# Strassen's scheme for the feed-forward gate and up projections of a five-mixer network on one core

## The reference, cut to what matters

```python
D_MODEL, SEQ, DEPTH = 1024, 512, 2
D_FF = 2816                      # ceil(8 * 1024 / 3 / 256) * 256

def _swiglu(h, w_gate, w_up, w_down):
    g = h @ w_gate.astype(h.dtype)
    u = h @ w_up.astype(h.dtype)
    return (jax.nn.silu(g) * u) @ w_down.astype(h.dtype)

h = _rmsnorm(x, norm_ffn_g[layer])
x = x + _swiglu(h, ffn_w_gate[layer], ffn_w_up[layer], ffn_w_down[layer])
```

## Time and profile before

| What | Value |
|---|---|
| median of three runs | 1898.31 us |
| span of the profiled execution, first to last instruction | 1895.7 us |
| PE / PEld / DVE / ACT / POOL busy | 99% / 79% / 57% / 42% / 8% |
| the two feed-forward blocks, by the starts of their first and next units | 215.49 to 575.97 us and 818.74 to 1179.22 us |
| mean granted TensorE clock | 0.999 |
| HBM traffic | 91 GB/s over the span |

### The profile page before, as it was taken

The page is one execution under the profiler, slowest core; times in us unless marked ns, Lnnn a source line. Parts: engine busy times, 40 slices in busy tenths (PEclk is TensorE's granted clock), DMA queues, the critical chain, the costliest instruction groups (busy, mean ns, idle before and its releaser), DMA issues.

```text
span 1895.7 us, 25382 instructions
## 1 busy us (share of the span) xinstructions
PE 1883.0 (99%) x9078; PEld 1504.8 (79%) x9078; DVE 1079.8 (57%) x1730; ACT 793.5 (42%) x1271; POOL 154.5 (8%) x234
## 2 busy tenths in 40 slices
PE   9999999999999999999999999999999999999998
PEld 7887888888888777788888888876777887777777
DVE  7787644433456676744443446576666565656553
ACT  6476432222234444533312334255655244445442
POOL 3111000000000000000000000000002054432000
PEclk9999999999999999999999999999999999999999
DMA  7333333323332122232322232212313232332222
GB/s 252 115 93 122 100 100 100 115 73 100 100 100 75 59 66 66 80 100 90 110 100 83 95 109 89 69 45 62 94 57 91 85 95 80 85 84 84 82 89 73
DMA packets 53855, 173.78 MB, mean 92 GB/s; under 512 B 7392, under 2 KB 15712, under 8 KB 53776
## 3 DMA queue, kind: packets, MB, share of 16 engines
q1 hardware_dynamic: 47408, 162.62, 27.0%
q0 software_dynamic: 6368, 10.13, 2.3%
HBM read 168.51 MB, written 4.21 MB: 91 GB/s over the span
## 4 chain that ended last, share of the span: by engine, by line
PE 96%; DVE 1%; ACT 1%; DMA 1%; issue 1%; DVEq 0%; ACTq 0%; SPq 0%
PE ps L494 17%; PE ps L496 17%; PE ps L495 17%; PE sc L494 6%; PE sc L495 6%; PE sc L496 6%; PE tr L495 4%; PE tr L496 4%; PE tr L494 4%; PE ps L683 3%; PE tr L649 3%; PE sc L606 2%; PE ps L606 1%; PE sc L654 1%; PE ps L670 1%; DMA Wr<-in_w 1%
## 5 line engine op out<-in xcount | busy, mean ns | idle before, releaser
L1090 ACT ACTIVATE Wh<-Wr 128x1024 fp32r<-128x1024 f32 (+2 forms) x268 | 300.1, 1120 | 638.4 <-PE ps L496 284.2
L494 PE MATMUL ps<-Hl,Wh 128*128 128x512 f32 x1136 | 465.6, 410 | 0.0
L496 PE MATMUL ps<-Hh,Wh 128*128 128x512 f32 x1136 | 444.0, 391 | 0.0
L495 PE MATMUL ps<-Hh,Wl 128*128 128x512 f32 x1136 | 443.2, 390 | 0.0
L1550 DVE TENSOR_TENSOR Wl<-Wr,Wh 128x1024 fp32r<-128x1024 f32 (+2 forms) x268 | 352.2, 1314 | 139.5 <-ACT Wh L1090 138.2
L494 PEld LDWEIGHTS ps<-Hl,Wh 128*128 128x128 f32 x1136 | 213.4, 188 | 53.8 <-issue 11.1
L496 PEld LDWEIGHTS ps<-Hh,Wh 128*128 128x128 f32 x1136 | 213.3, 188 | 46.7
L495 PEld LDWEIGHTS ps<-Hh,Wl 128*128 128x128 f32 x1136 | 213.9, 188 | 39.4 <-issue 0.5
L494 PE MATMUL sc<-Hl,Wh 128*128 128x512 f32 x432 | 168.6, 390 | 0.0
L495 PE MATMUL sc<-Hh,Wl 128*128 128x512 f32 x432 | 168.1, 389 | 0.0
L496 PE MATMUL sc<-Hh,Wh 128*128 128x512 f32 x432 | 168.1, 389 | 0.0
(11 more groups left out here) (334 smaller groups left out, 2662.5 us busy)
## 6 DMA issues: line engine op xcount, KB each, us to landing
Wr<-in_w SPq DMA_DIRECT2D x228, 512.0 KB, 3.5
Wr<-in_w SPq DMA_DIRECT2D x32, 768.0 KB, 4.3
Wr<-in_w SPq DMA_DIRECT2D x16, 640.0 KB, 3.8
scr<-in_rpb POOLq DMA_DIRECT2D x128, 24.0 KB, 2.2
X<-in_x SPq DMA_DIRECT2D x8, 256.0 KB, 4.3
Wr<-in_wri SPq DMA_DIRECT2D x4, 512.0 KB, 3.5
out_t<-X SPq DMA_DIRECT2D x8, 256.0 KB, 2.4
scr<-d_rel POOLq DMA_DIRECT2D x8, 192.0 KB, 3.9
```

The lines of the kernel that those rows point to most:

```text
L494: pe.matmul(bank[:, 0:n], hi, rl[:, k, :], start=(k == 0), stop=False)
L495: pe.matmul(bank[:, 0:n], lo, rh[:, k, :], start=False, stop=False)
L496: return pe.matmul(bank[:, 0:n], hi, rh[:, k, :], start=False, stop=(k == kc - 1))
L1090: act.activation(place(Wh, slot, kc), place(Wr, slot, kc), ACT.Copy).then_inc(w_hi, 1)
```

## The change

A gate unit and an up unit of one hidden chunk are now one **pair**. With the weights as A11, A12 (gate, input chunks of even and of odd number), A21, A22 (up, the same) and the activations as B11, B12 (even chunks, left and right 256 tokens), B21, B22 (odd chunks), the four 128 x 256 results are made by seven block products (Winograd's form of Strassen's scheme). One block product is four chunks of 128 x 128 weights times 256 columns, three TensorE products each: 12 products of 256 columns.

The operands are sums. Per pair GpSimd makes four sums of weight blocks, each 128 x 512: S3 = A11 - A21, S1 = A21 + A22, S2 = S1 - A11, S4 = A12 - S2. Of the activations, VectorE makes T1 (even chunks, right minus left), T2, T3, T4 once per layer, in `out_proj`, and they are split as `Eh`, `El`. ScalarE and VectorE now split A11 with A12 (128 x 1024), A22 (128 x 512) and the four sums (128 x 512 each) of every pair, and A21 not by itself.

The results are added up outside TensorE: ScalarE copies two partial banks to SBUF (`first_of`, 512 columns, `last_of`, 256 columns), and VectorE makes four reads of 256 columns from PSUM, three of them an addition of a copied part (`read`, `third_read`), one with the factor `rt` (`rows_right`); the left half of the gate gets the factor by itself (`rows_left`). A pair's last two products run during the next pair, and its Silu, gating and split during the one after that.

The sums of squares of the two feed-forward norms move from VectorE to GpSimd. The first unit of each down projection is no longer a unit of its own: its steps are put between the last two block products of the last pair. The down projections use PSUM banks 6 and 7. GpSimd's DMAs after the feed-forward blocks are issued after them. SyncE loads a pair with two DMAs of 512 KB into one of two buffers that are kept until the pair's last sum is made.

The core of the diff, TensorE first:

```diff
+                def product(w, t, out, begins=False, steps=range(4)):
+                    hi, lo = weights(Wh, w), weights(Wl, w)
+                    for j in steps:
+                        th, tl = quarter(t, j)
+                        cs = slice(j * P, (j + 1) * P)
+                        pe.matmul(out, hi[:, cs], tl, start=(begins and j == 0), stop=False, skip_group_check=True)
+                        pe.matmul(out, lo[:, cs], th, start=False, stop=False, skip_group_check=True)
+                        mm = pe.matmul(out, hi[:, cs], th, start=False, stop=(j == 3), skip_group_check=True)
+                    return mm
...
+                def first_pair():
...
+                    if ready:
...
+                        pe.wait_ge(h_ok, SPLITS[norm] + 7)
+                        product("A11", "B11", alpha, True)
+                        product("A12", "B21", beta_, True, range(3))
+                        pe.wait_ge(el_ok, 4 * (p0 // 22) + 3)
+                        product("S3", "T3", delta, False, range(3))
+                        pe.wait_ge(h_ok, SPLITS[norm] + 8)
+                        product("A12", "B21", beta_, False, range(3, 4)).then_inc(p2_ok, 1)
+                        pe.wait_ge(el_ok, 4 * (p0 // 22) + 4)
+                        product("S3", "T3", delta, False, range(3, 4)).then_inc(w_used, 2)
+                        mean_square(norm, later=True)
+                    else:
+                        product("S3", "T3", delta, True)
+                        product("A12", "B21", beta_).then_inc(p2_ok, 1)
+                        product("A11", "B11", alpha, True).then_inc(w_used, 2)
+                    pe.wait_ge(w_lo, b + lo_at["A22"])
+                    pe.wait_ge(dc_ok, 2 * p0 + 1)
+                    product("A22", "T4", delta).then_inc(w_used, 1)
...
+                def pair(g, par, at_end=False):
...
+                    def fifth():
+                        pe.wait_ge(w_lo, b + prior["S1"])
+                        pe.wait_ge(e_ok, 4 * p0 + prior_read["r2"])
+                        product("S1", "T1", alpha_b).then_inc(w_used, 1)
+
+                    pe.wait_ge(w_lo, b + lo_at["S3"])
+                    product("S3", "T3", delta, True).then_inc(w_used, 1)
...
+                    product("A12", "B21", beta_).then_inc(p2_ok, 1)
...
+                    product("A11", "B11", alpha, True).then_inc(w_used, 1)
+                    if not at_end:
+                        fifth()
...
+                    pe.wait_ge(dc_ok, 2 * g + (2 * p0 + 1))
+                    product("A22", "T4", delta).then_inc(w_used, 1)
...
+                    pe.wait_ge(e_ok, 4 * p0 + read["r1"])
+                    product("S2", "T2", alpha).then_inc(w_used, 1)
+                    pe.wait_ge(w_lo, b + prior["S4"])
+                    pe.wait_ge(e_ok, 4 * p0 + prior_read["r3"])
+                    product("S4", "B22", alpha_b).then_inc(w_used, 1)
...
+                down_steps(0, 2)
...
+                product("S1", "T1", alpha).then_inc(w_used, 1)
+                down_steps(2, 6)
...
+                product("S4", "B22", alpha).then_inc(w_used, 1)
+                down_steps(6, kc)
```

GpSimd's four sums (`lo_at` names the low split that frees each sum's buffer), and the adds of squares put among them:

```diff
+                    if step == 0:
...
+                        pool.wait_ge(w_lo, lo_at["S3"])
+                        pool.tensor_tensor(block4(sum3), gate[:, 0], up[:, 0], ALU.subtract).then_inc(sum_ok, 1)
+                    if step == 1:
+                        pool.wait_ge(w_lo, lo_at["S1"])
+                        pool.tensor_tensor(block4(sum1[par]), up[:, 0], up[:, 1], ALU.add).then_inc(sum_ok, 1)
+                    if step == 2:
+                        pool.wait_ge(w_lo, lo_at["S2"])
...
+                    if step == 3:
+                        pool.wait_ge(w_lo, lo_at["S4"])
...
+                    if part_ == "a":
+                        for m in range(6):
+                            add_square(norm, m)
+                        weight_sums(name, 0, 0, (0, 1))
+                        add_square(norm, 6)
+                        weight_sums(name, 0, 0, (2, 3))
+                        add_square(norm, 7)
```

ScalarE's order in one pair (`sum_hi` is the high split of a sum or block):

```diff
+                    if n != 0:
+                        sum_hi(name, g - 1, "S4", 1 - par, b + used["S4"])
+                    if n not in (0, 1) and not drain:
+                        silu()
+                    if more:
+                        sum_hi(name, g + 1, "S3", 1 - par, b + used["S3"])
...
+                        act.activation(first_of[par][:, :], ps[2 + par][:, :], ACT.Copy).then_inc(dc_ok, 1)
+                    if n not in (0, 1):
+                        y_hi_ffn()
...
+                        sum_hi(name, g + 1, "A", 1 - par, b + used["A"])
...
+                        sum_hi(name, g, "S1", par, b + used["S1"])
+                    act.wait_ge(w_used, b + used["A22"])
+                    act.activation(last_of[par], ps[2 + par][:, 0:256], ACT.Copy).then_inc(dc_ok, 1)
...
+                        sum_hi(name, g + 1, "A22", 1 - par, b + used["A22"])
+                        sum_hi(name, g + 1, "S2", 1 - par, b + used["S2"])
```

VectorE's order in one pair (`sum_lo` is the low split, which frees the sum's buffer):

```diff
+                    if n not in (0, 1):
+                        rows_right(g - 2, par, 6 * g + (b - 2))
...
+                    if n != 0:
+                        sum_lo(name, g - 1, "S4", 1 - par)
+                    if n not in (0, 1) and not drain:
+                        act_by_up(g - 2, par)
+                    if more and n != 0:
+                        sum_lo(name, g + 1, "S3", 1 - par)
+                    if n not in (0, 1):
+                        y_lo_ffn(g - 2, par)
...
+                    read(sq[:, par, left], ps[par], first_of[par][:, right])
...
+                    if more:
+                        sum_lo(name, g + 1, "A", 1 - par)
...
+                        third_read(g - 1, 1 - par, 6 * g + (b + (2 if last else 1)))
...
+                        sum_lo(name, g, "S1", par)
+                    if n != 0:
+                        rows_left(g - 1, 1 - par)
+                    if more:
+                        sum_lo(name, g + 1, "A22", 1 - par)
...
+                    read(up_of[par][:, left], ps[par], last_of[par])
...
+                        sum_lo(name, g + 1, "S2", 1 - par)
```

In `out_proj` ahead of a feed-forward block VectorE makes the sums of activation quarters (`even_quarters`, 256 columns; `odd_quarters`, 512 and 256 columns) and one more low split (`El`, 768 columns) per two chunks, and the splits of the first pair's S3, A and A22 stand behind chunks 5 and 6:

```diff
+                    if pairs_in and m == 5 and nrm:
+                        odd_lo(nrm, m)
+                        sum_lo(pairs_in, 0, "S3", 0)
+                    elif pairs_in and nrm:
+                        (odd_lo if m % 2 else even_lo)(nrm, m)
```

More of the change, by code:

```diff
@@ L107 @@
 SCALES = {n: i + 1 for i, n in enumerate(SPLITS)}
[L108 removed]
+OUT_BANK = {n: 6 if n.startswith("down") else 0 for n in X0}
 OUT_Y = {"rg_out": Y0["rg"], "sb_out": Y0["sb"], "even_out": Y0["even"], "odd_out": Y0["odd"]}
 OUT_KC = {"rg_out": KD, "sb_out": KD, "even_out": MIXC, "odd_out": MIXC}
+PAIR_OUT = {"gu0a": "rg_out", "gu0b": "down0a", "gu1a": "sb_out", "gu1b": "down1a"}
+DOWN_N = {"gu0a": 0, "gu0b": 1, "gu1a": 2, "gu1b": 3}
 AFTER = {"ffn0": "rg_out", "ffn1": "sb_out", "odd": "even_out"}
@@ L226, in program @@
         yt, xr, rf = acc, gx, rm
+        raw_w = [(part(7168, KD, P), part(8192, KD, P)),
+                 tuple(Wr[:, q, 0:KD * P].rearrange("p (k c) -> p k c", k=KD) for q in range(2))]
+        raw_rows = raw_w
+        raw_w = [[r.rearrange("p (j e) c -> p e j c", e=2) for r in two] for two in raw_w]
+        sum3, sum2 = scr[:, 9216:9728], scr[:, 9728:10240]
+        sum4 = [scr[:, 10240:10752], scr[:, 10752:11264]]
+        sum1 = [Wr[:, q, KD * P:MIXC * P] for q in range(2)]
+        tE = [gs[:, 0:768], ht.rearrange("p a b -> p (a b)")[:, 0:768]]
+        tO = [scr[:, 11264:12032], scr[:, 12032:12800]]
+        first_of = [rstd, acc]
+        last_of = [rm[:, 0:256], rm[:, 256:512]]
+        up_of = [gs[:, 0:S], gs[:, S:2 * S]]
         ring = [QT[:, 0, :], QT[:, 1, :], sq[:, 0, :], sq[:, 1, :]]
@@ L321, in four_heads, with load_pairs, load_pair @@
                 return a["w8"][first:first + 4].rearrange("m p c -> p m c")[:, :, 2 * P * (row % 4):2 * P * (row % 4 + 1)]
+            def load_pairs(name, b, row, pairs):
+                p0, landed = PAIR0[name], 8 * b - SKIP[name]
+                rows = a[f"w{KD}"].rearrange("u p (k c) -> u p k c", c=P)
+                def load_pair(h, par):
+                    for q in range(2):
+                        sp.wait_ge(w_in[q], 16 * h + landed)
+                        if h == 0:
+                            if name.endswith("a"):
+                                sp.wait_ge(x_ok, X0[PAIR_OUT[name]] + 1)
+                            else:
+                                sp.wait_ge(w_lo, b - 7)
+                        elif h == 1:
+                            sp.wait_ge(w_lo, b - 1 + q)
+                        else:
+                            sp.wait_ge(w_lo, b + 2 + q if h == 2 else 6 * h + (b - 12 + 2 * q))
+                            sp.wait_ge(sum_ok, 4 * h + (4 * p0 - 4))
+                        sp.dma_start(raw_rows[par][q], rows[2 * h + (row + q)]).then_inc(w_in[q], 16)
+                for h in range(pairs):
```

(19 more changed lines are left out.)

440 lines of the change are left out of this document (365 added, 75 removed).

## The result

The changed kernel takes 1939.05 us (median of 4 runs, 1937.24 to 1939.89), the kernel before 1898.21 (1897.88 to 1898.44) on the same chip: a ratio of 1.0215, 95% interval 1.0202 to 1.0227. I had forecast 1909 within 1876 to 1934, so the time lies outside the range, on the slow side. The profiled execution has a span of 1938.2 us, 42.5 more than before; I had forecast 11.3 more.

A forecast was written before the change was run, and what follows sets the result against it. TensorE was taken to bound the kernel, busy 99%. TensorE -35.2, holds +25.6, starts +14 and +2.8, ends +4.1 gave +11.3: span 1895.7 to 1907.0, with 2.6 carried 1909 us, range 1876 to 1934.

The forecast's parts named there:

- TensorE: Products of all 44 pairs: 10.08 us a pair in place of 10.88, 35.2 us gained at most.
- the period: Time from pair to pair, set by VectorE and GpSimd taking turns: 11.0 us, above TensorE's 10.08.
- the ends: Last pair's chain after its last product, in four places: 0.35 late in `a`, 1.7 in `b`, 4.1 us for four.
- the 3.9 of my sum: Turns per pair: GpSimd's four sums hold VectorE 4.40 us, less 0.68 under PSUM reads, plus 0.15 waiting.
- The rival on weight loads: Weight loads set TensorE's pace: a pair would take 15.8 us, +237, 2135 us in all; chance 0.03.
- Holds: In 32 pairs the period holds TensorE by 0.92 us each, 29.4 less 4 x 0.95: 25.6 us back.
- the 0.95 per group: Delay before a pair's third read that can be absorbed, once per group of pairs: some 0.95 us.
- Starts of `gu..a` (two): VectorE late for the first pairs of `gu..a`: 7 us each, 14 us for two.
- The stalls that I named: At a `gu..a` start: 5.8 us late first, A22 0.9, second pair's S3 2.1; 8.8 in strict turns, 7 taken.
- chunk 5 begins on time: In `rg_out`, VectorE's list before `gu..a` was counted only from chunk 5's add: 11.5 us, 20.3 with GpSimd's turns.
- GpSimd falling into VectorE's waits: In the pairs, GpSimd's sums run while VectorE waits: period near 10.25, -22 us, 1876 us in all; chance 0.28.
- A slower GpSimd (period 12.1): In the pairs, GpSimd's adds with cut-up operands are slower: period 12.1 us, +51, 1949 us in all; chance 0.12.

The follow-up runs named there:

- e1: The changed kernel with GpSimd's four weight sums per pair reading only 2 of every 128 columns and writing a constant over the rest: 1891.47 us, ratio 0.9964.
- e2: The changed kernel with the up unit and the gated product kept in PSUM: 1917.62 us, ratio 1.0103.
- e9: e2 with left row factors also in PSUM, rewritten starts, and VectorE's gate and up reads moved beside GpSimd's adds: 1891.80 us, ratio 0.9965.
- e4: The changed kernel with TensorE given 15 and 12 filler products in front of the sixth output unit and the first pair: 1937.51 us, ratio 1.0210.
- e5: e1 with GpSimd's adds of squares also reading only 8 of 512 columns and writing a constant over the rest: 1879.64 us, ratio 0.9906.
- e6: e5 with VectorE's quarter sums and their low parts also narrowed to 8 columns: 1875.57 us, ratio 0.9883.

## Why the prediction was wrong

**TensorE, the period, the ends.** Right. A pair without a wait is 10.07 us (forecast 10.08), a held one 11.05 (11.0), and e1, e2 and e9 show that the turns with GpSimd make the difference. The splits that stand behind the four sums are held by 1.10, 1.07, 1.11 and 0.75 us in the pair from 276 us on, 4.0 for the 3.9 of my sum. The last pair of a group runs free, the one before it nearly so (10.36). The rival on weight loads had no part: e1's pairs have as many loads. Holds came to 31.3 us for 25.6: 32 pairs at 0.98 for my 0.92, and next to nothing absorbed of the 0.95 per group that I took off. The rule of the Trainium skill's page "SBUF — State Buffer", section "SBUF: two separate sides", says the same of these turns: a VectorE operation with two SBUF inputs and a GpSimd operation that reads SBUF exclude each other for a whole instruction. The groups of 1.31 and 1.78 us in the change and of 0.69 in e1 agree.

**"Starts of `gu..a` (two)" is the step that failed**: 14 us, measured 39.4. What I counted in it was nearly right. VectorE's list from the add of chunk 5 to the last `El` was 20.3 us by my rows, in strict turns; the trace has it from 212.80 to 234.07, 21.3. The stalls that I named (first pair's rows, the last chunk's, A22's, the second pair's S3) come to 3.20 + 0.34 + 1.48 + 0.81 + 0.98 = 6.8 us in the first layer and 8.3 in the second, for the 7 that I took. What failed is the assumption that chunk 5 begins on time. The first four units of `rg_out` are finished at 196.0, when VectorE is at the second of their chunks, so four chunks wait for it, each with the quarters added to its list and two of them with a GpSimd add in their way (196.74 and 200.97, held by 0.8 and 0.6). They push back the split of the sixth unit: 3.92 us of stall. Behind the stalls products start 4.6 us later in sum at the lower clock, which belongs to the same lateness (e4 and the second layer): at the full clock TensorE would have waited that time. Another 2.6 us (1.57 + 0.30 + 0.71) went in the second pair, where TensorE waited for reads that VectorE did late, the first of them behind the row factor. I had counted neither the backlog, nor the clock, nor these reads.

By the runs the first layer's start of 19.0 us is made of 13.8 of turns with GpSimd (e5), some 2.1 of the quarters' own length (e6), and some 3 that are neither; what these 3 are stays open.

**The rivals.** GpSimd falling into VectorE's waits did not happen by itself, but e9 shows that its adds can be laid beside VectorE's reads from PSUM: its period is TensorE's. A slower GpSimd (period 12.1) did not come; its adds last 1.29 where they are not held. So the range was too narrow at the upper end for a reason that none of the rivals had: I gave the starts no range of their own above 9 each.

## What to carry to other kernels

When an operation is handed to GpSimd beside a busy VectorE, price it by the turns it takes from VectorE, 0.8 to 1.1 us for an add of 512 columns here, not by GpSimd's idle time; then put VectorE operations with a PSUM input beside it. When a list is summed up against another engine's work, begin the sum where the list begins, not where the late result is first needed: a backlog at the head is carried to the end. And a gain of 0.8 us per step pays only if the start of its loop costs less than the steps give.
